# Sample rows of the down projection: high and low parts side by side in one stationary tile

## The reference, cut to what matters

```python
def conv_ffn(h, conv_buf, w_up, conv_w, conv_b, w_down):
    u = h @ w_up
    ...
    a, b = jnp.split(c, 2, axis=-1)
    return (jax.nn.gelu(a) * b) @ w_down, u_ext[:, -(CONV_W - 1):]
...
    x = x + m @ w_o
    f, new_conv = conv_ffn(rmsnorm(x, norm2_g), conv_buf, w_up, conv_w, conv_b, w_down)
    return x + f, new_conv
```

## Time and profile before

| what | us |
|---|---|
| median of 3 runs | 2017.09 |
| lowest and highest of the 3 | 2016.33, 2020.13 |
| the profiled execution, its own time | 2018.43 |
| its span, first to last instruction | 2016.6 |
| PE busy, DVE busy, ACT busy | 1885.4 (93%), 989.9 (49%), 587.8 (29%) |
| mean granted TensorE clock | 0.967 |

### The profile page before, as it was taken

One profiled execution on the slowest core, in us unless ns is written; L12 is line 12 of the kernel. 1 busy time (PEld: TensorE's weight loads), 2 busy tenths in 40 slices (PEclk: granted clock), 3 DMA queues, 4 the chain that ended last, 5 costly groups with the idle time before them and its releaser, 6 DMA issues. The chain is left out here.

```text
span 2016.6 us, 30841 instructions
## 1 busy us (share of the span) xinstructions
PE 1885.4 (93%) x11702; PEld 1606.8 (80%) x11702; DVE 989.9 (49%) x1966; ACT 587.8 (29%) x982; POOL 117.3 (6%) x209
## 2 busy tenths in 40 slices
PE   7999999999787877998868999999999999999996
PEld 6777779999555555666658889999999999999995
DVE  5203442000364796566657274546545555555647
ACT  4211001211673585333322143122122123112213
POOL 0000000000100301332100001000000000000000
PEclk9999999999778799999979999999999999999998
DMA  6444447511712827999837115021112102102102
GB/s 220 169 169 170 174 169 282 198 56 45 198 4 77 320 92 284 381 383 393 325 132 250 49 53 162 22 62 55 38 31 62 41 22 62 42 21 62 42 11 107
DMA packets 138501, 274.14 MB, mean 136 GB/s; under 512 B 23625, under 2 KB 76506, under 8 KB 135898
## 3 DMA queue, kind: packets, MB, share of 16 engines
q1 hardware_dynamic: 116506, 154.33, 23.0%
q0 software_dynamic: 21888, 118.38, 16.0%
HBM read 243.24 MB, written 78.97 MB: 160 GB/s over the span
## 5 line engine op out<-in xcount | busy, mean ns | idle before, releaser
L2145 DVE TENSOR_TENSOR tl_x<-tl_x,tl_ps 128x512 f32<-128x512 f32 (+1 forms) x198 | 135.1, 687 | 194.8 <-PE tl_ps L2360 191.9
L499 PE MATMUL tl_ps<-tl_T_lo,tl_up_hi 128*128 128x364 f32 (+1 forms) x1008 | 222.2, 329 | 0.0
L499 PE MATMUL tl_ps<-tl_T_hi,tl_up_lo 128*128 128x364 f32 (+1 forms) x1008 | 222.2, 329 | 0.0
L499 PE MATMUL tl_ps<-tl_T_hi,tl_up_hi 128*128 128x364 f32 (+1 forms) x1008 | 222.2, 329 | 0.0
L499 PEld LDWEIGHTS tl_ps<-tl_T_hi,tl_up_hi 128*128 128x128 f32 x1008 | 174.9, 188 | 1.4
L499 PEld LDWEIGHTS tl_ps<-tl_T_hi,tl_up_lo 128*128 128x128 f32 x1008 | 174.8, 188 | 0.0
L499 PEld LDWEIGHTS tl_ps<-tl_T_lo,tl_up_hi 128*128 128x128 f32 x1008 | 174.7, 188 | 0.0
L469 PE MATMUL fr_ps<-fr_w_hi,h_hi 128*128 128x512 f32 x384 | 154.1, 401 | 2.6 <-DVE h_lo L365 2.6
L469 PE MATMUL fr_ps<-fr_w_hi,h_lo 128*128 128x512 f32 x384 | 152.8, 398 | 0.0
L469 PE MATMUL fr_ps<-fr_w_lo,h_hi 128*128 128x512 f32 x384 | 152.8, 398 | 0.0
L2360 PE MATMUL tl_ps<-tl_dn_lo,tl_f_hi 128*128 128x512 f32 x360 | 140.3, 390 | 0.0
(11 more groups left out here) (313 smaller groups left out, 3431.1 us busy)
## 6 DMA issues: line engine op xcount, KB each, us to landing
out_s<-in_cache POOLq DMA_DIRECT2D x8, 4080.0 KB, 20.3
all_lead<-in_w_up SPq DMA_DIRECT2D x44, 512.0 KB, 4.7
fr_raw<-in_w_in POOLq DMA_DIRECT2D x9, 2048.0 KB, 8.8
pg_pages<-in_pool POOLq DMA_DIRECT2D x64, 256.0 KB, 6.5
pg_pages<-in_pool SPq DMA_DIRECT2D x64, 256.0 KB, 7.4
pg_odds<-in_pool SPq DMA_DIRECT2D x64, 256.0 KB, 8.1
zs<-fr_zt SPq DMA_DIRECT2D x48, 256.0 KB, 2.0
tl_dn_raw<-in_w_down SPq DMA_DIRECT2D x22, 512.0 KB, 3.7
```

The costliest lines, as they stand in the source:

```text
L499: last = pe.matmul(out[:, n * 512:n * 512 + b - a], lhs, rhs[:, a:b], start=(i == 0), stop=(i == len(pairs) - 1))
L2145: dve.tensor_tensor(x, x, banks[m % len(banks)][0:n, :], ALU.add).then_inc(added, 1)
```

## The change

The stationary tile of the sample rows becomes 128 columns wide: the 64 columns of high parts, and beside them the 64 columns of low parts. One pass with the high down weights then gives high times high in PSUM partitions 0 to 63 and low times high in partitions 64 to 127. A second pass with the low down weights gives high times low in partitions 0 to 63 and, newly, low times low in partitions 64 to 127. So the two groups of that tile have 4 matmuls instead of 6, in the ten `down` calls; `last_down` stays as it is. DVE copies the 64 low columns beside the high ones after each low part is made (a wait on its own semaphore and a copy), TensorE waits for these copies before `down`, and the adds of that tile take 128 partitions instead of 64. The lower 64 partitions of `x2`'s ninth tile are set to zero once, ahead of the output projection's adds. After the tenth `down` SP moves these 64 rows of sums to partitions 0 to 63 by one DMA of 64 rows of 4 KB, and DVE adds them once, ahead of the last tile's `convolve_part(0)`.

```diff
-            (("f_hi", words(2, ROWS), F32R), ...
+            (("f_hi", words(2, ROWS + SROWS), F32R), ...
+        low = s.sb("low", [SROWS, D])
...
             next_down(FT - 1)
+            sp.wait_ge(added, END * (2 * RT) + 2)
+            sp.dma_start(low[:, :], x2[SROWS:P, QT, :]).then_inc(low_in, 16)
             sp.wait_ge(u_ready, 2 * FT)
...
-                dve.tensor_tensor(f_lo[:, u, :], c[:, 1, :], f_hi[:, u, :].bitcast(F32), ALU.subtract).then_inc(f_lo_done, 1)
+                dve.tensor_tensor(f_lo[:, u, :], c[:, 1, :], f_hi[:, u, 0:ROWS].bitcast(F32), ALU.subtract).then_inc(f_lo_done, 1)
+                dve.wait_ge(f_lo_done, j + 1)
+                dve.tensor_copy(f_hi[:, u, ROWS:ROWS + SROWS], f_lo[:, u, SEQ:ROWS].bitcast(F32)).then_inc(beside_done, 1)
 
             def add_down(i, t, banks):
-                n = rows_of(t)
+                n = P if banks is not end_banks else rows_of(t)
...
+            dve.memset(x2[SROWS:P, QT, :], 0.0).then_inc(low_zeroed, 1)
             for t in range(RT):
                 if t < 4:
                     rest_wo(4 + t)
...
             h_rest(RT - 1)
+            dve.wait_ge(low_zeroed, 1)
...
             rest_down(FT - 1, 1)
+            dve.wait_ge(added, END * (2 * RT) + 2)
+            dve.wait_ge(low_in, 16)
+            dve.tensor_tensor(x2[0:SROWS, QT, :], x2[0:SROWS, QT, :], low[:, :], ALU.add).then_inc(low_added, 1)
             convolve_part(0)
...
-            dve.wait_ge(added, END * (2 * RT) + 2)
+            dve.wait_ge(low_added, 1)
             dve.wait_ge(gain_f_in, 16)
...
                 pe.wait_ge(dn_lo_done, i * 2 + 2)
+                pe.wait_ge(beside_done, i * 2 + 2)
                 for t in range(RT):
-                    n = rows_of(t)
+                    if t < QT:
+                        passes = [(x[:, u, t * P:t * P + P], w) for u in range(2)
+                                  for x, w in ((f_hi, dn_hi[:, u, :]), (f_hi, dn_lo[u]), (f_lo, dn_hi[:, u, :]))]
+                    else:
+                        passes = [(f_hi[:, u, SEQ:ROWS + SROWS], w) for u in range(2) for w in (dn_hi[:, u, :], dn_lo[u])]
                     for k in range(2):
                         pe.wait_ge(added, i * (2 * RT) + 2 * t + k + 1)
-                        if n < P and not isinstance(i, int):
+                        if t == QT and not isinstance(i, int):
                             past_wait(pe, K)
...
-                            last = pe.matmul(dps[0:n, k * 512:k * 512 + 512], x, w[:, k * 512:k * 512 + 512],
-                                             start=(q == 0), stop=(q == 5))
+                            last = pe.matmul(dps[:, k * 512:k * 512 + 512], x, w[:, k * 512:k * 512 + 512],
+                                             start=(q == 0), stop=(q == len(passes) - 1))
                         last.then_inc(d_ready, 1)
```

More of the change, by code:

```diff
@@ L1769, in tail_stage @@
             (("wo1_hi", words(KD, HC), F32R), ("wo1_lo", words(KD, HC), F32R)),
-            (("f_hi", words(2, ROWS), F32R), ("f_lo", words(2, ROWS), F32R), ("dn_hi", words(2, D), F32R), ("dn_lo0", words(D), F32R)))
+            (("f_hi", words(2, ROWS + SROWS), F32R), ("f_lo", words(2, ROWS), F32R), ("dn_hi", words(2, D), F32R), ("dn_lo0", words(D), F32R)))
+        low = s.sb("low", [SROWS, D])
         cw, cb = s.sb("cw", [P, 3, 2 * FT]), s.sb("cb", [P, 2 * FT])
@@ L1794, in tail_stage @@
             "u_ready", "scaled", "tap", "conv_done", "gelu_done", "f_done", "f_hi_done", "f_lo_done", "d_ready", "added", "out_stored"))
+        low_zeroed, beside_done, low_in, low_added = (s.sem(n) for n in ("low_zeroed", "beside_done", "low_in", "low_added"))
         y_done, y_stored = s.sem("y_done"), [s.sem(f"y_stored{i}") for i in range(YS)]
@@ L1947, in head_f @@
                     act.wait_ge(d_ready, i * 2 * RT)
-                act.activation(f_hi[:, u, :], c[:, 1, :], ACT.Copy).then_inc(f_hi_done, 1)
+                act.activation(f_hi[:, u, 0:ROWS], c[:, 1, :], ACT.Copy).then_inc(f_hi_done, 1)
             def pair(i, more=True):
@@ L2350, in down @@
                 pe.wait_ge(dn_lo_done, i * 2 + 2)
+                pe.wait_ge(beside_done, i * 2 + 2)
                 for t in range(RT):
-                    n = rows_of(t)
+                    if t < QT:
[3 more added lines that the diff above has]
+                        passes = [(f_hi[:, u, SEQ:ROWS + SROWS], w) for u in range(2) for w in (dn_hi[:, u, :], dn_lo[u])]
                     for k in range(2):
                         pe.wait_ge(added, i * (2 * RT) + 2 * t + k + 1)
-                        if n < P and not isinstance(i, int):
+                        if t == QT and not isinstance(i, int):
                             past_wait(pe, K)
-                        passes = [(x[:, u, t * P:t * P + n], w, u) for u in range(2)
-                                  for x, w in ((f_hi, dn_hi[:, u, :]), (f_hi, dn_lo[u]), (f_lo, dn_hi[:, u, :]))]
-                        for q, (x, w, u) in enumerate(passes):
-                            last = pe.matmul(dps[0:n, k * 512:k * 512 + 512], x, w[:, k * 512:k * 512 + 512],
-                                             start=(q == 0), stop=(q == 5))
+                        for q, (x, w) in enumerate(passes):
+                            last = pe.matmul(dps[:, k * 512:k * 512 + 512], x, w[:, k * 512:k * 512 + 512],
+                                             start=(q == 0), stop=(q == len(passes) - 1))
                         last.then_inc(d_ready, 1)
```

## The result

| | before | changed |
|---|---|---|
| median of 15 runs, us | 2016.33 | 2006.23 |
| ratio, 95% interval | | 0.9950, 0.9937 to 0.9962 |
| profiled execution, its span | 2018.43, 2016.6 | 2004.48, 2002.7 |
| PE, DVE, ACT busy | 1885.4, 989.9, 587.8 | 1871.3, 996.6, 587.3 |

The change makes the kernel faster, by 0.5% (10.1 us between the medians; the forecast was 7.95). The time itself, 2006.23, lies 0.6 us under the range that was given, 2006.8 to 2012.0. One of the 15 runs of the kernel before is an outlier of 7801.2 us, without which the median is 2016.1.

What follows compares the result with a forecast made beforehand. TensorE was taken to bound the tail. Removed matmuls 9.45 us, less 1.4 for group 17's late release and 0.1 at the fold, gave 7.95 us saved: 2009.1 us from 2017.09, range 2006.8 to 2012.0.

Steps and rivals of the forecast that it cites:

- What bounds the kernel: Tail stage: TensorE alone sets the chain from 1095.90 to 1989.78 us; DVE takes over only for the last 27 us.
- the worth of a matmul: In `down`, 0.2269 us each by starts; the sample tile's 8 instead of 12 save 0.945 us per `down`, 9.45 for ten.
- Group 17: Sample tile's second group in `down`: waits for DVE's add of group 15, ending 0.02 us before due; loses 0.14 us each.
- the first rival: Sample tile's second group in `down` is released in time, so TensorE keeps its whole gain: 2007.7 us; chance 0.19.
- 1.4 us for ten: Predicted loss at the sample tile's second group over ten `down`, 0.14 us each, with ends of 0 and 0.26 each.
- The row it came from: Late release in the kernel before, near 1100.9 us: 0.26 us lost, 0.10 lateness and 0.16 signal and exposed weight load.
- The additions: Copies (about 0.5 us per product), zeros (1.23 us) and move (3.7 us) hidden at no cost; fold costs `last_down` 0.1 us.
- Sum: Whole kernel: 9.45 - 1.4 - 0.1 = 7.95 us saved.
- the ends of its own terms: Bounds of the unknown losses: sample tile's second group 0 to 0.26 us per `down`, fold 0 to 0.4; 2007.6 to 2010.6 us.
- the step from the sum to the range: Whole kernel time: unknown terms' 2007.6 to 2010.6 us widened by the runs' spread to 2006.8 to 2012.0.
- This term for the spread: Whole kernel time: lowest run 0.8 us under the median, profiled one 1.3 above it, used to widen the range.
- The base: Kernel before: median of three runs, 2017.09 us, from which the forecast time was reckoned.

Runs made afterwards that it cites:

- split: Changed kernel with the sample tile's two four-matmul groups apart, one first and one last in each `down`; ratio 0.9947 (0.9931 to 0.9963).
- no_past: Changed kernel without TensorE's semaphore step between the wait and the sample tile's matmuls in the loop; all ten `down` take 23.76 to 23.77 us.
- five_copies: Changed kernel with the copy of the 64 low columns made five times over; first `down` to `last_down` 694.11 us, against 694.12.
- late_move: Changed kernel with the move of the low sums issued when the last up projection ends; first `down` to `last_down` 702.48 us, tail 982.74 us.

## Why the prediction was right, and where it failed

*What bounds the kernel; the worth of a matmul.* Right. In split the eight matmuls of 128 columns run at the full tiles' pace and from the first `down` to `last_down` the kernel gets back 9.48 us, where the prediction had 9.45.

*Group 17.* The mechanism was right: the add ends 0.02 us before the due time, as forecast, the weight load is in the open, and the first rival (released in time) is out. The Trainium skill (TensorE: Matmul & The Clock Gate, Step-by-step: what each phase is for) has weight loads pulled ahead of matmuls in flight. Here that holds for the matmul before group 17 (load at 1792.97, matmul at 1793.19) but not behind the late wait: the load starts at 1793.52, after 0.36 us of idle time on PEld. Group 17 follows 1.04 us after group 16's start, recorded with 0.47 us, where the prediction had 0.9 to 1.0 and 0.5. The size was off: **"1.4 us for ten"** was 2.2, since a `down` lasted 23.82 to 23.83 us nine times and 23.77 once against 23.60 without the wait (9 x 0.22 + 0.17). The row it came from has no semaphore step behind its wait, and the loop has one, worth 0.06 us; without it 0.17 are left (no_past, 23.77), against the 0.14 of the prediction.

*The additions.* Copies, zeros and move cost nothing and the fold 0.1, as forecast. For the copies five_copies shows it; for the zeros, written between the tail's first matmul and the first `down`, this stretch is 237.12 us against 237.13 before (averages over the twelve profiles: 237.4 with them, 237.2 without, within the scatter). A copy with its wait takes 0.23 us and not the 0.5 that were charged. The move took 5.8 us instead of 3.7, inside its bounds.

*Sum.* 7.25 in the chain instead of 7.95, inside the ends of its own terms (6.5 to 9.45); nearly all of the difference is the term of group 17.

*Where it failed: the step from the sum to the range.* "The lowest run is 0.8 under the median and the profiled one 1.3 above it, so the range is 2006.8 to 2012.0." This term for the spread, 0.8 us down and 1.3 up, was mis-sized. It was taken from three runs and a profile, and the stages ahead of the tail, with the same work in all twelve profiles, end anywhere within 8.6 us. The medians of the changed kernel in three comparisons are 4.1 us apart: 2006.23, 2010.3 and 2008.55. The base was off as well: the 2017.09 of three runs became 2016.33 with fifteen, and 2014.59 and 2014.17 in the later comparisons. In the first comparison the spread added to the change and the time fell 0.6 us below the range; that the other two lie inside it is as much luck. The ratio's mean over the three comparisons agrees with the chain.

## What to carry to other kernels

Where groups alternate between two buffers, shortening two neighbours shortens the time that the consumer has for the buffer between them: with the short groups apart (split) the whole gain arrived. A wait that ends at the due time isn't free: here it cost the weight load that did not run ahead and the semaphore step between wait and matmul. And before a range is set, find which part of the execution varies: here a change of 0.4% was exact in the chain of one profile and needed three comparisons in the timed runs.

## What was not expected of the hardware

The stretch from the first `down` to `last_down` repeats to 0.01 us over executions (701.37 three times without the change, 694.12 to 694.13 three times with it), while the stages between 510 us and the tail vary by some 8 us, and the granted clock there with them. A semaphore step on TensorE, free behind an early wait, costs 0.06 us behind a late one. And the move of 256 KB from SBUF to SBUF took 5.1 to 6.2 us in the seven profiles that issue it right behind the last down weights, and 3.0 in the one that issues it 14 us later (late_move); what makes the difference was not tested.
